# Two-layer blocks on one core: the shift of three RMS norms is taken into the rounding, the root of each norm comes in two parts

## The reference, cut to what matters

```python
def rms_norm_2(x, g):
    xf = x.astype(jnp.float32)
    y = xf * lax.rsqrt(jnp.mean(xf * xf, axis=-1, keepdims=True) + EPS)
    return (y * g.astype(jnp.float32)).astype(x.dtype)

def modulate(x, g, mod, i):
    return rms_norm_2(x, g) * (1 + mod[:, :, i + 1]) + mod[:, :, i]
```

## Time and profile before

| | |
|---|---|
| median of 3 runs | 3304.61 us (3302.58 to 3310.13) |
| time of the profiled execution | 3304.75 us |
| its span, first to last instruction | 3303.0 us |
| TensorE busy | 3107.6 us (94%) |
| DVE busy | 1632.8 us (49%) |
| ACT busy | 1238.2 us (37%) |
| mean granted TensorE clock | 0.969 of full speed |

### The profile page before, as it was taken

The page is one execution under the profiler, slowest core; times in us unless marked ns, Lnnn a source line. Parts: engine busy times, 40 slices in busy tenths (PEclk is TensorE's granted clock), DMA queues, the critical chain, the costliest instruction groups (busy, mean ns, idle before and its releaser), DMA issues. The chain is left out here.

```text
span 3303.0 us, 39562 instructions
## 1 busy us (share of the span) xinstructions
PE 3107.6 (94%) x15192; PEld 2483.6 (75%) x15192; DVE 1632.8 (49%) x2422; ACT 1238.2 (37%) x2046; POOL 155.1 (5%) x142
## 2 busy tenths in 40 slices
PE   6989999999998999998998998999999898899999
PEld 5666677776776677776885777788888775778887
DVE  4763666665454566674415543433333615344344
ACT  2543233335563233336114442423222424543332
POOL 2200000011000000000002001000000100000000
PEclk9969999999999999999998999999999999999999
DMA  5101443433201434431201001112121120022221
GB/s 189 52 25 40 178 157 136 177 106 52 77 1 58 175 124 178 152 109 39 64 26 52 1 1 52 51 51 76 51 76 51 51 77 0 1 77 102 102 87 65
DMA packets 157679, 259.17 MB, mean 78 GB/s; under 512 B 54332, under 2 KB 70074, under 8 KB 157436
## 3 DMA queue, kind: packets, MB, share of 16 engines
q1 hardware_dynamic: 155812, 252.66, 21.8%
q10 hardware_dynamic: 1628, 4.76, 0.4%
q0 software_dynamic: 128, 0.26, 0.0%
HBM read 255.57 MB, written 2.10 MB: 78 GB/s over the span
## 5 line engine op out<-in xcount | busy, mean ns | idle before, releaser
L1250 ACT ACTIVATE w_hi<-wbuf 128x1024 fp32r<-128x1024 f32 (+1 forms) x349 | 368.1, 1057 | 1227.4 <-PE psA L777 1163.9
L775 PE MATMUL psA<-act_hi,w_hi 128*128 128x512 f32 (+1 forms) x1872 | 707.5, 378 | 62.4 <-DVE act_lo L1929 37.1
L1923 DVE TENSOR_TENSOR w_lo<-wbuf,w_hi 128x1024 fp32r<-128x1024 f32 (+1 forms) x349 | 429.3, 1233 | 556.2 <-ACT w_hi L1250 551.0
L776 PE MATMUL psA<-act_lo,w_hi 128*128 128x512 f32 (+1 forms) x1872 | 701.4, 375 | 0.0
L777 PE MATMUL psA<-act_hi,w_lo 128*128 128x512 f32 (+1 forms) x1872 | 700.5, 374 | 0.0
L775 PE MATMUL psA<-hid_hi,w_hi 128*128 128x512 f32 (+1 forms) x1280 | 476.8, 373 | 5.4 <-DVE work L2032 4.5
L776 PE MATMUL psA<-hid_lo,w_hi 128*128 128x512 f32 (+1 forms) x1280 | 472.1, 369 | 0.0
L777 PE MATMUL psA<-hid_hi,w_lo 128*128 128x512 f32 (+1 forms) x1280 | 471.4, 368 | 0.0
L775 PEld LDWEIGHTS psA<-act_hi,w_hi 128*128 128x128 f32 x1872 | 358.8, 192 | 134.7 <-issue 52.1
L777 PEld LDWEIGHTS psA<-act_hi,w_lo 128*128 128x128 f32 x1872 | 357.7, 191 | 62.7
L776 PEld LDWEIGHTS psA<-act_lo,w_hi 128*128 128x128 f32 x1872 | 359.0, 192 | 60.9 <-issue 0.2
(11 more groups left out here) (271 smaller groups left out, 3562.8 us busy)
## 6 DMA issues: line engine op xcount, KB each, us to landing
wbuf<-in_mlp_w_dram SPq DMA_DIRECT2D x64, 2048.0 KB, 8.2
work<-in_ada_w_dram SPq DMA_DIRECT2D x32, 1536.0 KB, 10.9
wbuf<-in_ab_w_in_dram SPq DMA_DIRECT2D x10, 1024.0 KB, 5.0
wbuf<-in_ple_w_gate_dram SPq DMA_DIRECT2D x4, 2048.0 KB, 7.6
wbuf<-in_hy_w_in_dram SPq DMA_DIRECT2D x3, 2048.0 KB, 13.6
wbuf<-in_c_w_in_dram SPq DMA_DIRECT2D x3, 2048.0 KB, 7.6
wbuf<-in_hy_w_out_dram SPq DMA_DIRECT2D x2, 2048.0 KB, 7.8
wbuf<-in_mla_w_out_dram SPq DMA_DIRECT2D x2, 2048.0 KB, 8.3
```

The costliest lines, as they stand in the source:

```text
L775: pe.matmul(psA[:, s, a:b], w_hi, x_hi[:, a:b], start=first, stop=False)
L776: pe.matmul(psA[:, s, a:b], w_hi, x_lo[:, a:b], start=False, stop=False)
L1250: return nc.scalar.activation(out, in_, func, **kw)
L1923: tt(split_target(wL, stage, u), unit(v, stage, u, g), split_target(wH, stage, u), ALU.subtract).then_inc(S["w_split"], 1)
```

## The change

For norms 0, 1 and 3 (`direct` = `KD` tiles) ACT no longer writes a shifted copy. It reads the scaled tile and writes the rounded sum of tile and shift, one operation for each part of the tokens. DVE takes the rest by a scalar_tensor_tensor, (scaled + shift) - hi, also one for each part. Norm 2 (`direct` = 0) keeps the shift in place, the Copy and the tensor_tensor rest.

For all four norms Ln and Exp are done first for the latent columns and then for the context columns. DVE may scale the latent part of tile 0 after the first half (`root_part`). DVE's order is new for all of them: scaling (0, latent), scaling (0, context), scaling (1, latent), rest 0, scaling (1, context), scaling 2, rest 1, and so on. With 512 tokens there is no context part, and the order is as before. `raw_part` and `hi_part` are the semaphores of the latent parts where there are two.

```diff
--- before.py
+++ after.py
@@ -269,7 +269,7 @@
         stage_over = sem("stage_over")
         out_set, out_stored = sem("out_set"), sem("out_stored")
         S = {n: sem(n) for n in (
-            "centered", "squared", "sum_ready", "sum_read", "mean_read", "acc_set", "acc_mean", "ple_set", "tile_sum", "norm_set", "acc_zero", "relu_used", "gate_used", "act_hi", "act_split", "w_hi", "w_split", "g_hi", "hidden_set",
+            "centered", "squared", "sum_ready", "sum_read", "mean_read", "acc_set", "acc_mean", "ple_set", "tile_sum", "root_part", "raw_part", "hi_part", "norm_set", "acc_zero", "relu_used", "gate_used", "act_hi", "act_split", "w_hi", "w_split", "g_hi", "hidden_set",
             "ada_used", "ada_sum", "row_ready", "row_set", "row_turned", "conv_set", "vec_set", "sqrt_set", "lam_exp", "lam_set",
             "dsa_max", "mla_max", "sw_max", "cat_max", "rope_raw", "root_set", "head_sq",
             "onat_set", "kr_set", "rot_set", "rot_used", "log_set", "row_arg", "carry_arg", "decay_masked", "decay_set", "gain_set", "query_set",
@@ -1325,9 +1325,9 @@
                     if u >= 2 and evacuate:
                         evacuate(u - 2)
 
-            def shift_and_split(first, x, spans, shift, x_hi=None, n=None, behind=None):
-
-                for k in range(KD):
+            def shift_and_split(first, x, spans, shift, x_hi=None, n=None, behind=None, start=0):
+
+                for k in range(start, KD):
                     act.wait_ge(S["norm_set"], first + k + 1)
                     for a, b, e in spans:
                         ins = f(x[:, k, a:b], x[:, k, a:b], ACT.Identity, bias=shift(k, e))
@@ -1366,6 +1366,7 @@
                 return square
 
             def rms(i, layer, first, n, dst, x_hi=None, ahead=()):
+                direct = 0 if i == 2 else KD
                 if i % 2 == 0:
                     for k in range(KD if i else 0):
                         act.wait_ge(S["residual_set"], k + 1)
@@ -1374,13 +1375,27 @@
                     w_hi(*a)
                 spans = [(0, LAT, 0)] + ([(LAT, n, 1)] if n > LAT else [])
                 if i % 2 == 0:
-                    inverse_root(f"rms{i}", 0, rstd[:, 0:n], n, eps_rms)
+                    ps, read = get_a(act, f"rms{i}", 0)
                 else:
                     act.wait_ge(S["sum_ready"], 2 + (i + 1) // 2)
-                    f(rstd[:, 0:n], psO[:, 0:n], ACT.Ln, bias=eps_rms)
+                    ps, read = psO, S["sum_read"]
+                for a, b, _ in spans:
+                    f(rstd[:, a:b], ps[:, a:b], ACT.Ln, bias=eps_rms)
                     act.drain()
-                    f(rstd[:, 0:n], rstd[:, 0:n], ACT.Exp, scale=-0.5).then_inc(S["sum_read"], 1)
-                shift_and_split(rms_squares[i], dst, spans, lambda k, e: mod[:, layer, first * KD + k, e:e + 1], x_hi, n)
+                    f(rstd[:, a:b], rstd[:, a:b], ACT.Exp, scale=-0.5).then_inc(read if b == n else S["root_part"], 1)
+
+                def shift(k, e):
+                    return mod[:, layer, first * KD + k, e:e + 1]
+
+                for k in range(direct):
+                    for a, b, e in spans:
+                        if b < n:
+                            act.wait_ge(S["raw_part"], direct * i + k + 1)
+                        else:
+                            act.wait_ge(S["norm_set"], rms_squares[i] + k + 1)
+                        f(x_hi[:, k, a:b], dst[:, k, a:b], ACT.Identity, bias=shift(k, e)).then_inc(
+                            S["act_hi"] if b == n else S["hi_part"], 1)
+                shift_and_split(rms_squares[i], dst, spans, shift, x_hi, n, start=direct)
 
             def ple(l):
                 def gate(j):
@@ -1968,20 +1983,46 @@
                 v.drain()
                 for a in ahead:
                     w_lo(*a)
+                direct = 0 if i == 2 else KD
+                hi, lo = (sH[n], sL[n]) if hi is None else (hi, lo)
+                spans = [(0, LAT, 0)] + ([(LAT, n, 1)] if n > LAT else [])
+
+                def scaled(k, a, b, e):
+                    ins = stt(dst[:, k, a:b], xT[:, k, a:b], aff[:, k, e:e + 1], rstd[:, a:b], ALU.mult, ALU.mult)
+                    if b == n:
+                        ins.then_inc(S["norm_set"], 1)
+                    elif k < direct:
+                        ins.then_inc(S["raw_part"], 1)
+
+                def rest(k):
+                    if k >= direct:
+                        x_lo(split, k, dst, hi, lo)
+                        return
+                    for a, b, e in spans:
+                        if b < n:
+                            v.wait_ge(S["hi_part"], direct * i + k + 1)
+                        else:
+                            v.wait_ge(S["act_hi"], BASE_X[split] + k + 1)
+                        ins = stt(lo[:, k, a:b], dst[:, k, a:b], mod[:, layer, first * KD + k, e:e + 1], hi[:, k, a:b], ALU.add, ALU.subtract)
+                    ins.then_inc(S["act_split"], 1)
+
+                if n > LAT:
+                    v.wait_ge(S["root_part"], i + 1)
+                    scaled(0, *spans[0])
                 if i % 2 == 0:
                     emptied(v, f"rms{i}", 0)
                 else:
                     v.wait_ge(S["sum_read"], (i + 1) // 2)
-                hi, lo = (sH[n], sL[n]) if hi is None else (hi, lo)
-                spans = [(0, LAT, 0)] + ([(LAT, n, 1)] if n > LAT else [])
-                for k in range(KD):
-                    for a, b, e in spans:
-                        ins = stt(dst[:, k, a:b], xT[:, k, a:b], aff[:, k, e:e + 1], rstd[:, a:b], ALU.mult, ALU.mult)
-                    ins.then_inc(S["norm_set"], 1)
-                    if split and k >= 1:
-                        x_lo(split, k - 1, dst, hi, lo)
-                if split:
-                    x_lo(split, KD - 1, dst, hi, lo)
+                scaled(0, *spans[-1])
+                scaled(1, *spans[0])
+                rest(0)
+                if n > LAT:
+                    scaled(1, *spans[1])
+                for k in range(2, KD):
+                    for span in spans:
+                        scaled(k, *span)
+                    rest(k - 1)
+                rest(KD - 1)
 
             def residual(stage, mix):
                 def add(m):
```

## The result

| | before | changed |
|---|---|---|
| median of 22 runs each | 3305.91 us (3302.51 to 3313.67) | 3311.58 us (3309.49 to 3315.77) |
| span of the profiled execution | 3303.0 us | 3313.9 us |
| mean granted TensorE clock | 0.969 | 0.963 |

The ratio is 1.0017, with a 95% interval of 1.0011 to 1.0023: the changed kernel is slower by about 5.7 us, where 2.9 us less was forecast. The measured 3311.58 lies outside the range of 3297.5 to 3306.0.

The account below looks back on a forecast made before the run. TensorE, busy 94% of the span, was taken to bound the kernel, idling at the norms for their rests. -1.55 - 1.55 + 0.85 - 0.64 = -2.9 us, from a median of 3304.61 to 3301.7 us; range 3297.5 to 3306.0.

Parts of the forecast that it names:

- Norms 0 and 1, -1.55 each: In norms 0 and 1 TensorE goes on with tile 7 at 18.85 instead of 20.40 us, bound by rest 7's supply.
- The rest's price: DVE's scalar_tensor_tensor rest takes 746 ns for 512 columns; a 768-token rest costs 1.07 us of queue instead of 0.88.
- the other estimate of the prediction for this piece: DVE's rest by the page's formula (N+151)/0.96 ns: 0.69 us for 512 columns, the sum within 0.3 us per norm.
- The *slower* rival: DVE's rest runs at 1.47 times the forecast's time everywhere, 0.5 us more per tile: +6.7 us, 3311.3; chance 0.04.
- Norm 2, a loss of 0.85: In norm 2 the new order makes tile 1's shift and rest 7 1.37 us late; TensorE loses 0.85 us.
- Norm 3, -0.64: In norm 3 TensorE starts at 2935.76 instead of 2936.40, then its own work binds: gain 0.64 us.
- The bounds of its terms: Ranges for the norms' terms, such as 1.0 to 1.9 gain in norm 0; stated span -1.5 to -4.5 us.
- The rival that the clock holds through the norms: TensorE stays at 2.4 GHz after the norms' shorter idle times; norm 3 gains at most 1.2 more: 3300.5; chance 0.08.
- The step that failed: In the sum over the kernel, added waits and three more semaphores cost nothing, or a few tenths of a us.
- something outside: An effect from elsewhere than the norms, such as a shifted weight transfer, moves the time; no size given, chance 0.03.
- The last of the prediction's own signs of being wrong: The forecast is wrong if the whole span moves by more than the norms' own stretches do; no size given.

Follow-up runs that it names:

- one drain: The changed kernel with one more drain, which does no work, on DVE in norm 0: 3298.20 us, 0.9976 of the kernel before.
- norm 0 only: The kernel before with only norm 0 in its changed form, norms 1, 2 and 3 as before: 3315.53 us, ratio 1.0026.
- eight drains: The kernel before with 8 drains, which do no work, added on DVE in norm 0: 3317.36 us, ratio 1.0033.
- nine drains: The kernel before with 9 drains, which do no work, added on DVE in norm 0: 3306.51 us, ratio 1.0.
- changed kernel with nine drains: The changed kernel with 9 more drains on DVE in norm 0, in its wait for the root: 3299.35 us, 0.9976 of the kernel before.
- six copies: The kernel before with six small copies on DVE after the last latent row's division in the window attention: 3317.64 us, ratio 1.0036.

## Why the prediction was wrong

- **Norms 0 and 1, -1.55 each: right in norm 0, nearly so in norm 1.** Start 4.6 forecast, 4.62 and 4.60 measured. Rest 7 forecast at 18.81 and measured at 18.64 and 18.61. Gain 1.65 in norm 0. In norm 1 it is 20.38 - 19.05 = 1.33, as TensorE reached tile 7 after rest 7 had landed: its own work bound, where the forecast had the supply.
- **The rest's price: right.** 746 ns was taken for 512 columns, and 0.75 us is in the rows; the other estimate of the prediction for this piece, 0.69 by a formula, was too low. The *slower* rival, which put it at 1.47 times 746 ns, did not happen. That its 3311.3 us is close to the measured 3311.58 is chance.
- **Norm 2, a loss of 0.85: right.** The shift of tile 1 was forecast at 6.33, measured 6.22, rest 7 at 21.71, measured 21.61. TensorE goes on with tile 7 at 2657.78 - 2636.12 = 21.66 after the Ln, where it was 20.92: 0.74.
- **Norm 3, -0.64: right at the start**, 3.88 against 4.52. The prediction says that nothing else holds TensorE in this norm. But later it waits for a weight rest, 0.47 us at 2961.47, and it did so before. There the lateness is 11.83 us, at the Ln of this norm 12.34, so 0.51 us of the gain are kept. The four norms together gain 1.65 + 1.33 - 0.74 + 0.51 = 2.75 us, where 2.9 was forecast. (The bounds of its terms add up to -1.2 and -4.4, not to the -1.5 and -4.5 that it states; nothing rests on this.)
- **The rival that the clock holds through the norms did not happen.** TensorE still restarts at the lower level; its first product of norm 0 takes 0.76 us, as before.
- **The step that failed** is in the sum: "Added waits and three more semaphores issue beside other work: nothing, or a few tenths." What the waits and semaphores cost where they stand was indeed small. But the sum has no term for what the eight more DVE instructions of norm 0 do further on: they move DVE's later code, and one instruction of the window attention was then issued 0.35 us late. It delayed TensorE in a part where it has 0.23 us of idle time anyway, and the granted clock fell for 41 us: 9 to 11 us by the medians, 13 at the Ln of norm 1 in the trace. The effect was counted in "something outside", at 0.03. The last of the prediction's own signs of being wrong, that the whole span moves by more than the norms' stretches do, is the one that showed. The sign was wrong by this: with the place moved by one more instruction the change measures -8.5 us by the medians.
- **Explained in part:** that -8.5 is more than the -2.9 of the norms. The trace with one drain is only 4.5 us shorter than before (3298.5 against 3303.0): its execution lies 2.0 us above the median of its kernel (3300.24 against 3298.20), that of before 2.0 below the median beside it (3304.75 against 3306.74). Of the 4.5 some 2.75 are the norms, and the shorter stretch after 1646 is part of the rest. The other 4 us lie in executions without a trace. Their mean granted clock is 0.969 or more in all ten runs with one drain, and from 0.965 to 0.971 in the 23 of before. Half-clock stretches of a few us differ among all traces, and which of them make up the remainder isn't shown.
- **Not explained:** why DVE issues one instruction late. The runs show that its place in the code decides, to within one instruction, and the traces that the late places lie multiples of 128 instructions apart (last section), but neither shows the mechanism. And they don't show by which measure the clock falls: 0.23 and 0.40 us of idle time at the place left it up, and with 0.58 and 0.78 it fell.

## What to carry to other kernels

When a local edit moves the time the wrong way, subtract the two traces by the same instruction before arguing about the edit: here the loss lay 430 us behind it. Here one instruction 0.35 us late was enough to bring a part with many small matmuls to half clock for 41 us, so look at the granted clock of such parts first whenever code ahead of them grows or shrinks. To tell an edit from its placement, add instructions without work to the kernel before, and one to the changed kernel, and run both with the edit.

## What the runs showed of the hardware

- One DVE instruction, after the last latent row of the window attention, had 0.53 us of issue idle in front of it when 8 instructions stood more ahead of it, and 0.17 or 0.18 with 0, 9 or 17 more.
- The late place is a number, not an instruction. Count DVE's instructions in the order in which a trace records them, drains and register instructions too. The late one is number 2884 in the changed kernel, with norm 0 only and with eight drains. With nine drains number 2884 is a drain that starts 0.38 us after the operation ahead of it instead of 0.03. It runs beside that operation, so nothing waits for it. In the kernel before another one is late, 384 numbers earlier: number 2500 is a drain that starts after 0.37 us instead of 0.02, and the operation behind it (L2429, at 1793.40) has 0.40 us of issue idle. With eight drains numbers 2500 and 3012 start after 0.41 and 0.42 us, where the same instructions take 0.07 with nine. In the changed kernel with nine drains number 2628 is late, and the operation behind it (L2465, at 1820.66) has 0.42 us of issue idle. So the places found, 2500, 2628, 2884 and 3012, lie multiples of 128 apart, and each lateness is about 0.35 us. At other numbers of this row none stands out in the traces; whether it is there and hidden by a wait is not shown.
- The half-clock stretch of 41 us began about 1 us after the idle time that went with it (1962 after 1960.80 in the changed kernel), and went on through units that, at full clock, had kept it up. The Trainium skill, "TensorE: Matmul & The Clock Gate", section "A second HAM failure mode: psum-queue depth-cycling", tells of short idle times between groups of matmuls that make the clock fall and rise. The traces agree in that short idle times can go with a fall. Here a single one was longer, 0.58 us where 0.40 had left the clock up, and the clock did not rise again for 41 us.
- Its price is about 0.3% of the kernel: with norm 0 only, with eight drains and with six copies the medians are 9.4, 10.6 and 10.9 us above before (the first with the gain of norm 0 in it).
